# Prompt attention on one core: attention outputs scaled by ScalarE in 40 of 64 steps, and a search round split around the row maximum

## The reference

```python
score = jnp.einsum('bqh,bqhs->bqs', wi, jax.nn.relu(logits)) * IDX_SCALE
score = jnp.where(key_pos <= q_pos, score, -jnp.inf)
_, sel = lax.top_k(score, topk)                       # topk = 256
...
s = jnp.einsum('bqhgd,bqkhd->bqhgk', q, k_sel) * (HEAD_DIM ** -0.5)
s = jnp.where(sel_valid, s, -jnp.inf)
p = jax.nn.softmax(s, axis=-1)
o = jnp.einsum('bqhgk,bqkhd->bqhgd', p, v_sel)
```

## Time and profile before

| | |
|---|---|
| median of 3 runs | 2813.49 us (2811.13 to 2814.82) |
| profiled execution, its time | 2821.48 us |
| its span | 2819.7 us |
| PE busy | 2684.9 us (95%) |
| DVE busy | 1484.1 us (53%) |
| ACT busy | 844.1 us (30%) |
| POOL busy | 109.4 us (4%) |
| mean granted TensorE clock | 0.982 |

### The profile page before, as it was taken

The page is one execution under the profiler, slowest core; times in us unless marked ns, Lnnn a source line. Parts: engine busy times, 40 slices in busy tenths (PEclk is TensorE's granted clock), DMA queues, the critical chain, the costliest instruction groups (busy, mean ns, idle before and its releaser), DMA issues. The chain is left out here.

```text
span 2819.7 us, 44920 instructions
## 1 busy us (share of the span) xinstructions
PE 2684.9 (95%) x17434; PEld 2558.0 (91%) x17434; DVE 1484.1 (53%) x2831; ACT 844.1 (30%) x1506; POOL 109.4 (4%) x135
## 2 busy tenths in 40 slices
PE   7999899789999999999999989979999999999997
PEld 7899755567899999999999989979999999999997
DVE  6679788896434444444444454352544444444444
ACT  5556576464313111111111141230411111111110
POOL 1300133000000000000000000000000000000000
PEclk9899999999999999999999999999999999999998
DMA  5313589500111111111111111111111111111111
GB/s 191 95 41 89 198 317 382 196 1 1 31 37 46 45 42 41 44 45 45 45 45 45 45 38 46 43 30 45 34 42 44 45 45 45 45 45 45 45 45 64
DMA packets 182247, 197.95 MB, mean 70 GB/s; under 512 B 14325, under 2 KB 154871, under 8 KB 173943
## 3 DMA queue, kind: packets, MB, share of 16 engines
q1 hardware_dynamic: 170279, 120.91, 14.2%
q0 software_dynamic: 11776, 75.50, 7.1%
q10 hardware_dynamic: 80, 0.02, 0.0%
HBM read 184.69 MB, written 11.73 MB: 70 GB/s over the span
## 5 line engine op out<-in xcount | busy, mean ns | idle before, releaser
L578 DVE TENSOR_TENSOR trunk_xT<-ffn_acc,trunk_xT 128x364 f32<-128x364 f32 x528 | 272.7, 533 | 164.5 <-PE ffn_acc L646 164.3
L646 PE MATMUL ffn_acc<-ffn_act_hi,trunk_w_hi 128*128 128x364 f32 (+1 forms) x1056 | 346.4, 328 | 3.5 <-DVE ffn_act_lo L544 3.5
L646 PE MATMUL ffn_acc<-ffn_act_lo,trunk_w_hi 128*128 128x364 f32 (+1 forms) x1056 | 348.0, 330 | 0.0
L646 PE MATMUL ffn_acc<-ffn_act_hi,trunk_w_lo 128*128 128x364 f32 (+1 forms) x1056 | 346.1, 328 | 0.0
L634 PE MATMUL ffn_acc<-ffn0x_x_hi,trunk_w_hi 128*128 128x364 f32 (+1 forms) x1032 | 338.5, 328 | 1.2 <-DVE ffn_norm_tmp L552 1.2
L634 PE MATMUL ffn_acc<-ffn1x_x_hi,trunk_w_hi 128*128 128x364 f32 (+1 forms) x1032 | 338.5, 328 | 1.2 <-DVE ffn_norm_tmp L552 1.2
L634 PE MATMUL ffn_acc<-ffn0x_x_hi,trunk_w_lo 128*128 128x364 f32 (+1 forms) x1032 | 338.4, 328 | 0.0
L634 PE MATMUL ffn_acc<-ffn1x_x_hi,trunk_w_lo 128*128 128x364 f32 (+1 forms) x1032 | 338.4, 328 | 0.0
L634 PE MATMUL ffn_acc<-ffn0x_x_lo,trunk_w_hi 128*128 128x364 f32 (+1 forms) x1032 | 338.0, 328 | 0.0
L634 PE MATMUL ffn_acc<-ffn1x_x_lo,trunk_w_hi 128*128 128x364 f32 (+1 forms) x1032 | 338.0, 328 | 0.0
L493 ACT ACTIVATE trunk_w_hi<-trunk_w_raw 128x1024 fp32r<-128x1024 f32 x130 | 136.7, 1051 | 415.1 <-PE ffn_acc L646 415.1
(11 more groups left out here) (407 smaller groups left out, 5150.8 us busy)
## 6 DMA issues: line engine op xcount, KB each, us to landing
trunk_w_raw<-in_ffn_w_gu SPq DMA_DIRECT2D x88, 512.0 KB, 3.9
trunk_w_raw<-in_ffn_w_down SPq DMA_DIRECT2D x44, 512.0 KB, 3.7
trunk_w_raw<-in_sg_w_in SPq DMA_DIRECT2D x16, 512.0 KB, 3.9
attxm_w_raw<-in_att_w_in SPq DMA_DIRECT2D x14, 512.0 KB, 6.1
search_row_buf<-r_kept SPq DMA_DIRECT2D x10, 512.0 KB, 3.7
x_kept<-x_xT SPq DMA_DIRECT2D x8, 544.0 KB
trunk_xT<-x_kept SPq DMA_DIRECT2D x8, 544.0 KB, 8.1
att_proj<-in_x_prompt SPq DMA_DIRECT2D x8, 512.0 KB, 7.5
```

The lines of the kernel that those rows point to most:

```text
L578: nc.vector.tensor_tensor(xT[:, o, a:a + w], banks[e % 6][:, 0:w], xT[:, o, a:a + w], ALU.add).then_inc(drained, 1)
L646: last = nc.tensor.matmul(banks[e % 6][:, 0:w], part[:, t * 512 + o * P:t * 512 + (o + 1) * P], (a_hi, a_lo)[m][:, t, a:a + w], start=(t = ...
```

## The change

In positions up to 40, the output of step s-1 is scaled by ACT instead of DVE, for s-1 = 0 to 39 (the tiles 0 to 4). ACT does it behind its copy of the turned probabilities and ahead of `copy_out(s-2)` and `exps(s+2)`. The one semaphore `o_scaled` becomes two, and `wait_scaled` picks the one that a step needs. In the hosting positions `next_level` and the marking of tile 7 (`flag`) now stand ahead of `tops(s+2)` on DVE, and the counting of tile 6 (`tally`) behind it. The other two searches of the kernel call `compare`, which is `flag` and then `tally`, as before.

```diff
     def compare(self, nc, dve, n):
+        self.flag(nc, dve, n)
+        self.tally(nc, dve, n)
+
+    def flag(self, nc, dve, n):
         for r in self.by_act:
             nc.vector.tensor_scalar(self.hit[r][:, :], self.sets[r][0], self.level[:, r:r + 1], None,
                                     ALU.is_ge).then_inc(self.compared, 1)
+
+    def tally(self, nc, dve, n):
         for r in self.by_dve:
...
+    by_act = starts[5]
...
+        def wait_scaled(eng, s):
+
+            if s < by_act:
+                eng.wait_ge(o_by_act, s + 1)
+            else:
+                eng.wait_ge(o_by_dve, s - by_act + 1)
...
             def turn_out(s):
-                pe.wait_ge(o_scaled, s + 1)
+                wait_scaled(pe, s)
...
                 if s:
-                    pe.wait_ge(o_scaled, s)
+                    wait_scaled(pe, s - 1)
...
+            def scale_out(s):
+                act.wait_ge(pv_ready, s + 1)
+                act.wait_ge(rtotal_ready, s + 1)
+                if s >= 2:
+                    act.wait_ge(o_turned, s - 1)
+                nc.scalar.activation(o_rows[:, s % 2, :], out[:, 0:HD], ACT.Copy, scale=rtotal[:, s % 2:s % 2 + 1]
+                                     ).then_inc(o_by_act, 1)
+
...
                         copy_group(act, j, lambda o, i: nc.scalar.activation(o, i, ACT.Copy))
+                if 1 <= s <= by_act:
+                    scale_out(s - 1)
                 if s >= 2:
                     copy_out(s - 2)
...
                 if s >= 2:
-                    dve.wait_ge(o_scaled, s - 1)
+                    wait_scaled(dve, s - 2)
                 nc.vector.reciprocal(rtotal[:, s % 2:s % 2 + 1], total[:, s % 2:s % 2 + 1]).then_inc(rtotal_ready, 1)
-                if s:
+                if s > by_act:
                     scale_out(s - 1)
-                if s + 2 < n_steps:
-                    tops(s + 2)
                 if s in round_at:
                     n = round_at[s]
                     if n > FOREGONE:
                         late.next_level(nc, dve, n - 1)
-                    late.compare(nc, dve, n)
+                    late.flag(nc, dve, n)
+                if s + 2 < n_steps:
+                    tops(s + 2)
+                if s in round_at:
+                    late.tally(nc, dve, round_at[s])
```

More of the change, by code:

```diff
@@ L2118, in prompt_attention_stage @@
         out, o_tr = S.ps("out", [P, 512]), S.ps("o_tr", [P, 512])
-        (scored, ntop_ready, exp_ready, rtotal_ready, turned, pv_ready, o_scaled, o_turned, o_copied) = (
-            S.sem(n) for n in ("scored", "ntop_ready", "exp_ready", "rtotal_ready", "turned", "pv_ready", "o_scaled",
+        (scored, ntop_ready, exp_ready, rtotal_ready, turned, pv_ready, o_by_act, o_by_dve, o_turned,
+         o_copied) = (
+            S.sem(n) for n in ("scored", "ntop_ready", "exp_ready", "rtotal_ready", "turned", "pv_ready", "o_by_act", "o_by_dve",
                                "o_turned", "o_copied"))
@@ L2272, in scale_out @@
                 nc.vector.tensor_scalar(o_rows[:, s % 2, :], out[:, 0:HD], rtotal[:, s % 2:s % 2 + 1], None,
-                                        ALU.mult).then_inc(o_scaled, 1)
+                                        ALU.mult).then_inc(o_by_dve, 1)
             tops(0)
```

## The result

The changed kernel takes 2819.94 us (median of 12 runs, 2815.94 to 2825.53) against 2813.59 us before (12 runs, 2811.11 to 2815.21). The ratio is 1.0024, 95% interval 1.0016 to 1.0032: 6.8 us slower, 4.5 to 9.0. The forecast was 4.4 us slower, 2817.9.

A forecast was written before the change was run, and what follows sets the result against it. DVE was taken to bound the hosting stretch, PE the rest. PE entering its own regime 4.0 us late plus 0.4 in tile 0 made 4.4 us slower, from the median 2813.49 to 2817.9; range 2812.5 to 2822.0.

The forecast's parts named there:

- What bounds: Prompt-attention stage: DVE sets the pace in the hosting stretch (busy 80.10 of 83.80 us), PE before and after it.
- The scaling: Hosting stretch: moving it relieves DVE of 26 x 0.25 = 6.5 us; on ACT each costs 0.37 us, less 0.10 overlap.
- The ring: Each hosting round: level, marks, maximum, exponential, count wait in a circle, 3.88 us at 640 wide, 3.16 at 256; chance 0.81.
- the signs named beforehand: New profile: level idle 0.2 to 1 us nearly every round, pair 7.0 us, DVE under 85%, step 38 about 4 us later.
- the handover from ACT back to DVE: Each round, from ACT's count read-out to DVE's next level: taken as 0.05 us, near the 0.04 of the other direction.
- The sum along the stretch: Hosting positions: 0.8 us ahead at position 23's level, 2.8 behind at 37's, PE's own regime entered 4.0 us late.
- the early marks: Start of the hosting stretch: the first marks no longer wait for the maximum and run in the 0.56 us before it.
- tiles 0 and 2: Where PE is the bound: ACT scaling behind its copy costs 0 to 0.6 us in tile 0, taken as 0.4; tile 2 has room.
- the scaling of step 37 behind ACT's last count: Position 38: this scaling releases PE's values of step 38 at 632.4 us instead of 628.37.
- DVE goes on setting the pace: Rival, hosting stretch: DVE's saving counts in full, -6.5 + 0.4 us, time 2807.4, faster; chance 0.06.
- the two effects cancel: Rival, hosting rounds: 0.2 us less per round gives back 4.4 us over 22 rounds, time stays 2813.5; chance 0.1.
- The clock: Rival, hosting stretch: PE, less busy, has its granted clock fall towards 0.57, 30 us more, 2848; chance 0.03.

The follow-up runs named there:

- scaling only: Kernel before, with only the scaling of steps 0 to 39 moved to ACT and the round in its old order; ratio 0.9986, stage 206.14 us.
- the split alone: Changed kernel with DVE scaling all outputs again, the round still split around the maximum; ratio 1.0024, stage 217.17 us.
- the ring cut: Split round with ACT's count ahead of the exponential: ratio 0.9981 with the scaling on ACT, 0.9994 with all scalings on DVE.
- a dose in it: Changed kernel with one extra DVE copy per round between the marks and the maximum; ratio 1.0035, stage 221.05 us.
- copy outside the ring: Changed kernel with one extra DVE copy per round behind the count of tile 6; ratio 1.0025, stage 217.57 us.
- count first, steps 12 to 39: Changed kernel with ACT's count ahead of the exponential and ACT scaling only steps 12 to 39; ratio 0.9977, stage 203.54 us.
- count first: Changed kernel with ACT's count of the round ahead of the exponential instead of behind it; ratio 0.9981, stage 204.00 us.

## Why the prediction was right, and where its size was off

**What bounds.** Right. DVE set the pace in the hosting stretch: relieved of its two scalings, a pair fell by 0.51 us (scaling only). PE set it elsewhere: from the level of position 37 on, the rest was 111.05 us in before and in the kernel with the scaling alone.

**The scaling.** Priced at 0.25 us on DVE, and at 0.37 on ACT by the nearest row with a pointer operand. The trace after has it at 0.35 to 0.37 (352 to 370 ns). The estimate by the Trainium skill (ScalarE: Activation LUTs, What ACT_TABLE_LOAD costs), 386 ns, is 16 to 34 ns high here.

**The ring.** The step that decided, and it held: with the split alone the slowdown is there, with the ring cut it is gone, with a dose in it most of the dose is paid. Of the signs named beforehand, the level waits for ACT's count 16 times (0.2 to 0.9 us, in 24 levels), the wait for the marks is gone, DVE's share is 84%, and from position 24 to 37 no maximum waits for PE. Four of the levels without idle time are those of positions 25, 29, 33 and 37, behind a 256-wide maximum and a copy of four blocks: there DVE's own list ends almost when the count is ready. With the copy outside the ring such a round takes 3.34 instead of 3.22 us, though DVE does 0.21 more, so the list is some 0.1 us shorter than the ring. The ring sums were 3.88 and 3.16; measured 3.95 and 3.22. The term that was mis-sized is the handover from ACT back to DVE, taken as 0.05 from the other direction. It is 577.35 - (577.05 + 0.19) = 0.11 us. In the 18 rings from position 13 to 17 and from 23 to 37, 0.06 more is 1.1 us of the 1.7 us of stage that were missed.

**The sum along the stretch.** To the level of position 13 it said 0.7 us gained (1.1 from the early marks, 0.4 lost in tiles 0 and 2): measured 0.2. With the split alone the gain is 0.8; the scaling's loss was put at 0 to 0.6 and is 0.46 to 0.62, and the start of the stage varies by a few tenths between executions with the granted clock there, which the prediction did not count. Up to the first 384-wide maximum, the kernels with DVE scaling these steps are alike; it comes 8.50 us in before (clock 0.69 in the first 5 us), 8.72 with the split alone (0.66) and 9.11 with count first, steps 12 to 39 (0.50). From 13 to 17: 1.1 predicted, 1.3 measured. From 17 to 23: 0.9 gained, 0.6 measured. From 23 to 37: 3.6 lost, 4.5 measured. The rest: 1.2 lost, 1.1 measured, but for another reason than the text gave for most of it. It blamed the scaling of step 37 behind ACT's last count; with the split alone, where DVE does that scaling, 0.7 of the 1.1 is still there. A level that is taken ahead of the maximum leaves that maximum behind it, 0.73 us from start to start at 640 wide (574.47 to 575.20): from the level of position 37 to that of 38 it is 3.64 us in before and 4.37 with the split alone. So the 0.8 us that the first early marks gained are given back at the last round. Only 0.35 is left for ACT's queue, and that the number of this term fits is luck.

**The rivals.** That DVE goes on setting the pace is excluded by the doses. The clock did not fall: 1.00 in the hosting stretch, with PE busy 68.92 of 88.60 us. The rule of the Trainium skill on half rate after waits between short bursts (TensorE: Matmul & The Clock Gate, HAM oscillation) does not show in this stretch, where PE's longest wait was 1.3 us. That the two effects cancel needed a ring 0.2 us shorter than its sum; it was 0.06 to 0.07 longer.

**The chances.** 0.66 stood on a change within 0.2%, and 0.28 on slower. The ratio came out just past that bound, 1.0024, its interval on both sides of it, so the result does not decide between the two.

**What stays open.** The gain of the split in positions 17 to 23 is 2.2 us with the scaling on ACT (17.58 to 15.41) and 1.4 with it on DVE (18.11 to 16.73). DVE's idle time around the two maxima goes from 3.3 to 0.9 us in the first case and from 2.1 to about 1 in the second, which is most of it, but how much comes from PE getting the scaling sooner (it waits 0.5 instead of 4.0 us for it with count first) was not run by itself. The granted clock at the start of the stage differs between executions (0.50 to 0.69 over 5 us); no run here was made to find out why.

## What to carry to other kernels

Moving work off the busiest engine and reordering what is left are two changes: run each alone. Before an operation is moved ahead of one that another engine waits for, follow the wait all the way round: if that engine's next result comes back to the moved operation, the two queues form a ring, and its sum, handovers included, is the new period. Where it is longer than the busiest engine's own list, either take an element out of it (here the count went ahead of the exponential) or leave the order as it was. The split is not bad in itself: with the ring cut it fills waits that the old order left empty.

## What the runs showed of the hardware

In this stage the handover from ACT to DVE is longer than from DVE to ACT: 0.11 us from the end of the read-out of an accumulator (577.24) to the waiting DVE instruction (577.35), against 0.03 from the end of the maximum (574.47 + 0.82 = 575.29) to the exponential that waits for it (575.32). Over the stage of the changed kernel it is 0.10 to 0.11 us in all 16 waits of the level for the count, and 0.03 to 0.04 us in the waits for the maximum. The first is always behind the read-out of an accumulator; no run here shows it behind another instruction of ACT.

A read-out of 0.19 us follows the activation that counts (577.05 in the changed kernel), as an instruction of its own. The level that waits for the count starts 0.11 us after the end of the read-out, so the read-out is a term of the ring.
